# One MLA layer's heads and joint attention: page transfers merged and spread, four high/low buffers, query and key-weight preparation moved a stage earlier

## The reference

```python
def mla_expand(ckv, kpe, w_ukv, g_k):
    kv = jnp.einsum('bnc,chd->bnhd', ckv, w_ukv.reshape(A_KV_LORA, A_HEADS, A_NOPE + A_V))
    k_nope, v = kv[..., :A_NOPE], kv[..., A_NOPE:]
    k_pe = jnp.broadcast_to(kpe[:, :, None, :], k_nope.shape[:-1] + (A_ROPE,))
    k = jnp.concatenate([k_nope, k_pe.astype(k_nope.dtype)], axis=-1)
    return rmsnorm(k, g_k), v

def mla_out(o, gate, w_out):
    b, s = o.shape[:2]
    return (o.reshape(b, s, A_WIDTH) * jax.nn.silu(gate)) @ w_out
```

## Time and profile before

| what | value |
|---|---|
| median of 3 runs | 2957.97 us (2957.61 to 2962.41) |
| the profiled execution | 2962.07 us |
| its span, first to last instruction | 2960.0 us |
| mean granted TensorE clock | 0.925 of 2.4 GHz |
| heads stages | 162.5 to 269.4 us and 2295.6 to 2402.7 us |
| attention stages, from SyncE's first issue | from 269.45 us and from 2402.74 us |
| pages in attention (start of the first and the last L1182 matmul) | 285.1 to 728.4 us and 2418.7 to 2861.8 us |

### The profile page before, as it was taken

One profiled execution on the slowest core, in us unless ns is written; L12 is line 12 of the kernel. 1 busy time (PEld: TensorE's weight loads), 2 busy tenths in 40 slices (PEclk: granted clock), 3 DMA queues, 4 the chain that ended last, 5 costly groups with the idle time before them and its releaser, 6 DMA issues. The chain is left out here.

```text
span 2960.0 us, 43156 instructions
## 1 busy us (share of the span) xinstructions
PE 2496.2 (84%) x15398; PEld 1967.5 (66%) x15398; DVE 1172.7 (40%) x1912; ACT 1043.6 (35%) x1793; POOL 713.2 (24%) x588
## 2 busy tenths in 40 slices
PE   3988899898869999998995958884969878998896
PEld 2955566665747778777785948873969455665656
DVE  3023455555324433443345242344141334554552
ACT  3043444443212332233323223554120534444431
POOL 4122222221312111221122322332321232222211
PEclk8998999999889999999997979997989889999998
DMA  2101233232210110011100111110111213323332
GB/s 88 57 31 32 81 92 86 78 90 75 86 51 29 44 37 31 21 44 45 37 16 9 57 34 31 34 32 24 36 38 49 88 40 95 87 77 91 90 112 86
DMA packets 113953, 167.31 MB, mean 57 GB/s; under 512 B 19530, under 2 KB 96332, under 8 KB 112100
## 3 DMA queue, kind: packets, MB, share of 16 engines
q1 hardware_dynamic: 113764, 164.84, 17.8%
HBM read 149.08 MB, written 15.70 MB: 56 GB/s over the span
## 5 line engine op out<-in xcount | busy, mean ns | idle before, releaser
L1759 PE MATMUL ps<-normed,w_slots 128*128 128x344 f32 x1152 | 358.2, 468 | 32.7 <-DMA w_slots<-in_w_hgrn 27.9
L1104 POOL TENSOR_TENSOR latents_t_lo<-latents_t,latents_t_hi 128x256 fp32r<-128x256 f32 x256 | 187.2, 732 | 692.2 <-ACT latents_t_hi L1323 689.6
L1759 PEld LDWEIGHTS ps<-normed,w_slots 128*128 128x128 f32 x1152 | 223.2, 198 | 147.7 <-issue 48.8
L1465 DVE TENSOR_REDUCE sums<-key_squares 128x8 f32<-128x512 f32 x256 | 175.5, 685 | 356.1 <-ACT key_squares L1330 356.1
L1182 PE MATMUL ps<-w_uk_hi,latents_t_hi 128*128 128x512 f32 x512 | 236.7, 462 | 85.2 <-POOL latents_t_lo L1104 73.9
L367 PE MATMUL ps<-src_hi,w_hi 128*128 128x344 f32 x1008 | 220.4, 328 | 102.4 <-POOL w_lo L338 102.4
L1330 ACT ACTIVATE key_squares<-ps 128x512 f32<-128x512 f32 x256 | 152.8, 597 | 299.8 <-PE ps L1182 298.5
L367 PEld LDWEIGHTS ps<-src_hi,w_hi 128*128 128x128 f32 x1008 | 174.6, 194 | 105.3 <-POOL w_lo L338 105.3
L367 PE MATMUL ps<-src_lo,w_hi 128*128 128x344 f32 x1008 | 218.2, 325 | 0.0
L367 PE MATMUL ps<-src_hi,w_lo 128*128 128x344 f32 x1008 | 216.6, 324 | 0.0
L1182 PE MATMUL ps<-w_uk_hi,latents_t_lo 128*128 128x512 f32 x512 | 207.2, 405 | 0.0
(11 more groups left out here) (295 smaller groups left out, 4575.8 us busy)
## 6 DMA issues: line engine op xcount, KB each, us to landing
pages<-in_pages SPq DMA_DIRECT2D x256, 144.0 KB, 2.1
latents_t<-in_pages_t SPq DMA_DIRECT2D x256, 128.0 KB, 2.0
w_slots<-in_w_hgrn SPq DMA_DIRECT2D x32, 512.0 KB, 4.2
w_slots<-in_w_mla_in SPq DMA_DIRECT2D x18, 512.0 KB, 3.3
w_slots<-in_w_rg SPq DMA_DIRECT2D x16, 512.0 KB, 3.5
residual<-in_x SPq DMA_DIRECT2D x4, 1032.0 KB, 6.9
residual<-in_x SPq DMA_DIRECT2D x1, 4128.0 KB, 13.6
x_home<-residual SPq DMA_DIRECT2D x1, 4128.0 KB, 15.6
```

The lines of the kernel that those rows point to most:

```text
L1104: nc.gpsimd.tensor_tensor(lat_lo[:, g % 2, :, :], lat_t[:, g % RING, :, :], lat_hi[:, g % 2, :, :].bitcast(F32), ALU.subtract).then_inc(lo ...
L1465: nc.vector.tensor_reduce(ss[:, b % 2, p, :], sq[:, g % 2, :].rearrange("p (h d) -> p h d", h=H), AX.X, ALU.add).then_inc(ssum, 1)
L1759: mm = nc.tensor.matmul(bank[:, 0:TT], ws[:, kind, kk, :], c.h[:, kk, t * TT:(t + 1) * TT], start=(kk == 0), stop=(kk == KD - 1))
```

## The change

It touches both stages.

1. The host packs a page's turned form as one row per partition: 256 latents, then the turned rotary keys (rows 0 to 31, zeros below), then the natural rotary keys. One transfer of 208 KB brings it (L1111 of the changed kernel). The natural copy holds latents alone, 128 KB.
2. Natural pages are issued four at a time, one part behind each group of turned pages, with a semaphore for each part.
3. GpSimd squares the rotary keys page by page (L1146) and no longer 16 pages at once (L1111 before).
4. High and low halves have four buffers each, and ScalarE makes the high half of page g+2 in page g (`LEAD`).
5. The absorbed queries and the two halves of the key weights are made in the heads stage; their buffers live through both stages. `wukt` is loaded there, into the buffer of `cq` squares.
6. Silu of the gate becomes x times exp(-log(1 + exp(-x))), three ScalarE passes and a GpSimd multiply for each block, placed in tiles 1 to 4 of the heads stage. The silu table and its load are gone.
7. In the heads stage the rotary-key matmuls come ahead of the sums for `ckv`, and the sums for `cq` behind the sample tile's queries.
8. `fold` and `spread` are issued behind the first four turned pages.

```diff
@@ mla_heads
             if spill is not None:
                 sp.dma_start(spill, c.x[:, :, :]).then_inc(spilled, 16)
+            sp.wait_ge(cq_summed, 1)
+            sp.dma_start(wukt, dram["w_uk_t"][j]).then_inc(wukt_landed, 16)
             sp.wait_ge(ckv_done, NKV)
...
+                if 1 <= i <= NG:
+                    pool.wait_ge(gate_steps, 3 * i)
+                    nc.gpsimd.tensor_tensor(m.gate[:, i - 1, :], m.gate[:, i - 1, :], sq_kv[:, i % 2, :], ALU.mult) \
+                      .then_inc(gated, 1)
+                if i == NG + 1:
+                    pool.wait_ge(wuk_split, 1)
+                    nc.gpsimd.tensor_tensor(m.wuk_lo[:, :, :], wuk[:, :, :], m.wuk_hi[:, :, :].bitcast(F32),
+                                            ALU.subtract)
...
             turn(NTILE - 1)
+            pe.wait_ge(wukt_landed, 16)
+            pe.wait_ge(qt_taken, 1)
+            pe.wait_ge(k_scaled, NTILE)
+            for h in range(H):
+                for k in range(NKV):
+                    mm = nc.tensor.matmul(K[:, (k * H + h) * NS:(k * H + h + 1) * NS], wukt[:, h, k * P:(k + 1) * P],
+                                          m.qs[0:NOPE, h, :], start=True, stop=True)
+            mm.then_inc(ql_summed, 1)
...
-            for k in range(NG):
-                nc.scalar.activation(m.gate[:, k, :], m.gate[:, k, :], ACT.Silu)
             load_ln_exp(nc)
...
+                if 1 <= i <= NG:
+                    gate = m.gate[:, i - 1, :]
+                    act.wait_ge(kv_rstd, 1)
+                    wait(act, gated, i - 2)
+                    nc.scalar.activation(sq_kv[:, u, :], gate, ACT.Exp, scale=-1.0).then_inc(gate_steps, 1)
+                    act.wait_ge(gate_steps, 3 * i - 2)
+                    nc.scalar.activation(sq_kv[:, u, :], sq_kv[:, u, :], ACT.Ln,
+                                         bias=c.const[:, C_ONE:C_ONE + 1]).then_inc(gate_steps, 1)
+                    act.wait_ge(gate_steps, 3 * i - 1)
+                    nc.scalar.activation(sq_kv[:, u, :], sq_kv[:, u, :], ACT.Exp, scale=-1.0).then_inc(gate_steps, 1)
@@ mla_attention, SyncE
-            for b in range(NS):
-                for group in range(4):
-                    ring(4 * b + group)
-                for part_ in range(4):
-                    natural(b, part_)
+            for group in range(NS * PAGES // GROUP):
+                transposed(group)
+                if group == 0:
+                    sp.dma_start(fold[:, :], dram["fold"]).then_inc(fold_landed, 16)
+                    sp.dma_start(spread[:, :, :], dram["spread"]).then_inc(p_loads, 16)
+                if group >= 3:
+                    natural((group - 3) // 4, (group - 3) % 4)
@@ mla_attention, ScalarE
             def latents_hi(g):
-                act.wait_ge(ring_landed[g % RING], 32 * (g // RING + 1))
-                wait(act, expanded, g - 1)
-                nc.scalar.activation(lat_hi[:, g % 2, :, :], lat_t[:, g % RING, :, :], ACT.Copy).then_inc(hi_done, 1)
+                act.wait_ge(ring_landed[g % RING], 16 * (g // RING + 1))
+                wait(act, expanded, g - DEPTH + 1)
+                nc.scalar.activation(lat_hi[:, g % DEPTH, :, :].rearrange("p k t -> p (k t)"),
+                                     ring[:, g % RING, 0:KVL], ACT.Copy).then_inc(hi_done, 1)
 
             def page(g):
-                if g + 1 < NS * PAGES:
-                    latents_hi(g + 1)
+                if g + LEAD < NS * PAGES:
+                    latents_hi(g + LEAD)
                 act.wait_ge(expanded, g + 1)
```

## The result

| | before | after |
|---|---|---|
| median | 2960.19 us (2957.61 to 2963.76, 4 runs) | 2871.57 us (2871.40 to 2871.70, 4 runs) |
| profiled execution, its span | 2962.07, 2960.0 | 2871.65, 2869.8 |
| mean granted TensorE clock | 0.925 | 0.937 |
| ratio of the times | | 0.9701, 95% interval 0.9685 to 0.9716 |

The account below looks back on a forecast made before the run. TensorE, busy 84%, was taken as the bound, with time to win where it stands still or runs at lower clock. Terms summed to 40.9 us a layer, 82 for both, giving a 2876 us median, range 2850 to 2914.

Parts of the forecast that it names:

- Long waits: TensorE's eight waits at first pages of samples, behind sixteen natural issues, would go with the spread: 19.5 us a layer.
- GpSimd's page squares: Rotary-key squares made page by page on GpSimd, 128 more small instructions a layer: cost 0.
- rival D: SyncE's order is not the cause; long waits stay, set by the ring's depth: 2926 us, chance 0.05.
- Clock behind the long waits: In the pages, TensorE's low clock after long waits goes with them: 8 us a layer, between 4 and 8.
- Short waits: Pages: four buffers and earlier high halves end TensorE's low-half waits, squares then release: 6.5 us a layer, ends 0 and 17.4.
- what is late next: Where long waits were, squares of the page before would be late, 0.7 us four times: -2.8 a layer.
- Start of the heads stage: Rotary keys start with the stage, silu's table and passes gone from there: 8 us a layer; 12 at full clock.
- Gate in the tiles: Heads stage: three ScalarE gate passes a tile, 3.3 us, hidden in its 3.63 us idle: 0, at most 13.2.
- Start of attention: First scores come 10.5 us behind the page table, TensorE waiting for `spread`: gain 4.7 us a layer, ends 2 and 7.
- Rival A: In the pages short waits go entirely, the clock holds and the heads start runs warm: 2852 us, chance 0.16.
- B: Only long waits go; heads stage gives nothing, start of attention stays bound by transfers: 2909 us, chance 0.19.
- C: Slower through the ring: turned pages of 208 KB land late, each of 62 groups waits: 2969 us, chance 0.03.

Follow-up runs that it names:

- Experiment 1: Changed kernel with a sample's sixteen natural pages again in one run, behind each fourth turned group: 2938.11 us, 0.9914 of before.
- experiment 2: Kernel before, with a sample's natural pages issued as two runs of eight, nothing else changed: 2966.43 us, 1.0014 of before.
- experiment 3: Kernel before, natural pages in fours, GpSimd's rotary squares taken from a block of the prompt's values instead: 2906.51 us, 0.9815 of before.
- Experiment 4: Changed kernel with two high/low buffers and the high half made one page ahead, as before: 2884.80 us, 0.9736 of before.
- experiment 7: Changed kernel with silu and its table load again at the heads stage's start, no gate passes in tiles: 2884.93 us, 0.9739 of before.
- squares first (5): Changed kernel, ScalarE taking the squares of page g before making the high half of page g+2: 2863.78 us, 0.9670 of before.
- `fold` first (6): Changed kernel with `fold` and `spread` issued ahead of the turned pages: 2868.33 us, 0.9676 of before.
- order back (8, first): Changed kernel, sums over `ckv` squares again ahead of the rotary keys on TensorE, ScalarE's rotary-key copy left early: 2884.85 us, 0.9741 of before.
- order back (8, second): Changed kernel, `ckv` sums again ahead of the rotary keys, ScalarE's rotary-key copies also back behind the `w_uq` scaling: 2882.24 us, 0.9733 of before.
- squares and `fold` first (9): Changed kernel with squares ahead of the high half on ScalarE and `fold` and `spread` ahead of the pages: 2860.43 us, 0.9653 of before.

## Why the prediction was right

**Long waits, 19.5 a layer: right in size, incomplete in cause.** Waits in the pages fell by 43.7 - 19.9 = 23.8 us, where 19.5 - 2.8 + 6.5 = 23.2 was forecast. Experiment 1 shows that the queue's order carries it. But the prediction gave the spread alone this power and set GpSimd's page squares at 0 as a cost. As a cost 0 is right (TensorE waits 0.8 us in 4 waits for a low half). What it missed is that page by page they are part of what makes the spread possible: in experiment 2, without them, a wait as long comes back on GpSimd, and in experiment 3, with the reader taken away, none is left. The prediction had not asked who else waits for the last natural page. It also read "the first page of a sample" where only every other sample's waits; the sum of the waits was right all the same. That rival D fell is shown by experiments 1 and 3.

**Clock behind the long waits, 8: the mis-sized term.** TensorE's busy time fell by 400.6 - 396.2 = 4.4 us, at the low end of the 4 to 8. The missing clock itself was read well enough, 15.9 to 6.1, so 9.8 less. The step that failed is "together miss 16 us of full clock", taken as 16 us of time. Missing clock costs nothing while TensorE stands idle (with each piece weighed by TensorE's busy time in it, only 6.2 of the 9.8 remain; the step from 6.2 to 4.4 stays open). Experiment 1 gives the same measure: 15.4 more of missing clock, 8.8 more of busy time. About half is the price here.

**Short waits, 6.5, and what is late next, -2.8: the reason held, both sizes were too large.** Squares became the releaser, in 62 waits. Experiment 4 has 13.2 us by the medians, but only 8.7 in waits and 8.9 in the pages, 4.4 a layer. Nothing was late next: where the long waits of the first layer were, pages 16, 48, 80 and 112 now wait for nothing. Before, TensorE stood 73.9 + 11.0 us for low halves and squares, 39.0 of it long; it now stands 35.9, so the short waits fell by 5.0 a layer where 6.5 - 2.8 = 3.7 was forecast. The two errors cancel in part. The pages of experiment 4 are also 1.6 us longer than those of experiment 3, which has two buffers as well, with 2.2 more of busy time; why was not followed.

**Start of the heads stage, 8: 10.9.** The term had two known ends, 8.1 at an unchanged pace and 12 at full clock, and the clock was 1.00 all through the first ten us. The prediction stayed with the pace of before, which has the low clock in it; the rotary keys, which follow the stage before with 1.60 us of idleness, show that here it does not fall. Over the whole stage 8.4 remain, since the 3.73 us of absorbed queries come at its end as forecast (-3). Experiments 7 and 8 undo one half each. Up to the sample tile's keys silu's place is worth 5.8 us and the order 3.7, 9.5 of the 10.9.

**Gate in the tiles, 0: right,** by the pitch of 9.05 and experiment 7. The cover of 3.63 is nearly used up.

**Start of attention, 4.7: 6.6.** The wait was the one foretold, but it ended 8.6 us behind the page table, not 10.5. The step that failed is "I take 3.1" for the first turned page, which went out after 2.2, and four pages took 3.7 instead of 4.3.

**The sum.** 40.9 a layer was forecast. The stretches give 8.4 + 6.6 + 28.1 = 43.1, against 5 + 4.7 + 31.2: two terms too small by 5.3 together and one too large by 3.1. Errors of both signs met, and the clock term, wrong by half, hid behind the heads stage. So that 88.6 us came near the 82 of the forecast is in part luck. Rival A named 2852: its warm start came true, its short waits did not go. B and C fell: no turned page is late once pages run, although a turned page of 208 KB lands in 2.6 us at the median and the kernel moves 7% more data (178.8 MB for 167.3).

## What to carry to other kernels

When a queue's long run of issues is spread, list every reader that waits for the run's last transfer, and what stands behind each on its engine; in the kernel before, with the run split in two, one such reader on GpSimd left no gain. Count what a buffer's lead puts ahead on an engine that works in order: a transfer that is late then stops more than the page it brings. Price a lower clock only where the engine is busy in it, and check it on a stretch: here a microsecond of missing clock cost about half a microsecond. A wait that names the squares or "issue" is followed to the engine whose own row ends just then.

## What was not expected of the hardware

The clock does not come back at a fixed moment after the start of attention. In every kernel here and in both layers it is 0.50 where the first scores begin. Then it comes back after very different times, as the missing clock of the pages tells (us):

| kernel | first layer | second layer |
|---|---|---|
| after | 6.1 | 6.2 |
| lead one (4) | 6.2 | 6.1 |
| squares first (5) | 1.9 | 6.1 |
| `fold` first (6) | 7.2 | 8.0 |
| silu back (7) | 1.7 | 5.7 |
| order back (8, first) | 1.7 | 2.0 |
| order back (8, second) | 6.1 | 6.2 |
| squares and `fold` first (9) | 7.2 | 5.3 |

In the change it stays at the lower level for about 12 us after 268.57, as its stretches show:

```profile
277.00:280.00 3.00, 2.68 (x8) 1.90 (x6) 0.08 (x1) 0.60 (x1) 0.93 (x2) 0.50 0.00 0
280.00:283.00 3.00, 2.92 (x31) 2.12 (x32) 1.52 (x5) 1.63 (x5) 0.70 (x2) 0.87 0.03 5
```

With the squares first, where the first scores are at 269.77, it is back after some 4 us in the first layer, and after some 12 in the second layer of the same execution, behind the same instructions:

```profile
272.00:275.00 3.00, 2.22 (x8) 1.31 (x7) 0.69 (x1) 0.90 (x2) 0.89 (x2) 0.75 0.64 184
275.00:278.00 3.00, 2.22 (x11) 1.49 (x9) 0.69 (x1) 1.39 (x5) 0.98 (x3) 1.00 0.00 0
```

Where the return is early TensorE's busy time is 393 us instead of 396. So a layer can win or lose 3 us by a clock that the edit does not touch. The gains of experiments 5 and 6 are known no better than that, and the losses of experiment 7 and the first of 8 are too small by 2.4 and 4.7 us, which their pages won back. What sets the moment stays open.
